# Mixer gate and output projections channel-major, with the gate blocks between the steps of the attention loops and x kept in DRAM meanwhile

## What is computed

```
proj = u @ w_in                      # 1024 -> 256 + 128 + 32 + 2304 + 1024 + 1024
c_q, c_kv, k_rope, qkv, gate_a, gate_b = split(proj)
o_mla = latent attention, 8 heads, all 512 keys per query
o_dil = three groups of windowed attention (dilation 1, 4, 16), 4 heads of 64 each,
        mixed by softmax over the groups' log-sum-exp
merged = sigmoid(gate_a) * (o_mla @ w_o_mla) + sigmoid(gate_b) * (o_dil @ w_o_dil)
y = merged @ w_out
x = x + gate * rms_norm(y, g_post_mix)
```

## Time and profile before

| | |
|---|---|
| median of 3 runs (lowest, highest) | 1302.97 us (1302.61, 1304.91) |
| span of the profiled execution | 1303.2 us |
| PE busy | 1206.4 us, 93% |
| DVE busy | 702.1 us, 54% |
| ACT busy | 508.7 us, 39% |
| mean granted clock of PE | 0.981 |
| chain that ended last, part of PE | 85% |
| mixer, from the last latent turn to the first chunk of w_out | 459.90 to 867.04 us |

### The profile page before, as it was taken

The page is one execution under the profiler, slowest core; times in us unless marked ns, Lnnn a source line. Parts: engine busy times, 40 slices in busy tenths (PEclk is TensorE's granted clock), DMA queues, the critical chain, the costliest instruction groups (busy, mean ns, idle before and its releaser), DMA issues.

```text
span 1303.2 us, 16470 instructions
## 1 busy us (share of the span) xinstructions
PE 1206.4 (93%) x5832; PEld 1013.2 (78%) x5832; DVE 702.1 (54%) x967; ACT 508.7 (39%) x844; POOL 38.7 (3%) x101
## 2 busy tenths in 40 slices
PE   2699999999999879899887799999899999999997
PEld 2688888888888767787777787887788888888885
DVE  6667777334584659923375666247632222226574
ACT  2431222224474547722354732336532222225542
POOL 3000000000010200010000000001100000000000
PEclk9999999999999979999899999999899999999999
DMA  7669999325545100023200213225233333336563
GB/s 310 208 188 280 277 278 282 104 75 183 185 170 186 47 15 25 26 81 98 81 1 1 66 65 116 95 81 177 82 97 97 97 97 97 97 97 193 178 196 111
DMA packets 132765, 167.36 MB, mean 128 GB/s; under 512 B 5735, under 2 KB 100074, under 8 KB 132714
## 3 DMA queue, kind: packets, MB, share of 16 engines
q1 hardware_dynamic: 132714, 166.68, 40.9%
HBM read 164.56 MB, written 2.10 MB: 128 GB/s over the span
## 4 chain that ended last, share of the span: by engine, by line
PE 85%; DVE 8%; ACT 3%; issue 2%; DMA 1%; POOL 0%; SPq 0%; POOLq 0%; ACTq 0%; DVEq 0%
PE ps L1743 27%; PE ps L1744 27%; PE ps L1745 27%; PE ps L1749 3%; DVE mla_pt_lo L1533 1%; DVE stat L1520 1%; DVE mla_p L1527 1%; DVE h_lo L1175 1%; DVE upd L1189 1%; PE ps L2204 1%; DMA x_resid<-in_x 1%; DVE w_lo L1121 1%; ACT h L711 0%; DVE ada_acc L1189 0%; PE ps L1781 0%
## 5 line engine op out<-in xcount | busy, mean ns | idle before, releaser
L1121 DVE TENSOR_TENSOR w_lo<-w_raw,w_hi 128x1024 fp32r<-128x1024 f32 (+2 forms) x240 | 286.2, 1209 | 232.1 <-ACT w_hi L656 228.8
L656 ACT ACTIVATE w_hi<-w_raw 128x1024 fp32r<-128x1024 f32 (+2 forms) x240 | 246.4, 1045 | 243.9 <-PE ps L1745 221.5
L1743 PE MATMUL ps<-h_hi,w_hi 128*128 128x512 f32 (+1 forms) x768 | 289.0, 376 | 10.2 <-DVE h_lo L1175 10.2
L1744 PE MATMUL ps<-h_lo,w_hi 128*128 128x512 f32 (+1 forms) x768 | 287.5, 374 | 0.0
L1745 PE MATMUL ps<-h_hi,w_lo 128*128 128x512 f32 (+1 forms) x768 | 287.5, 374 | 0.0
L1743 PEld LDWEIGHTS ps<-h_hi,w_hi 128*128 128x128 f32 x768 | 147.2, 192 | 36.0 <-DVE h_lo L1175 11.2
L1230 DVE TENSOR_TENSOR a_buf<-silu,ps 128x512 f32 (+1 forms) x44 | 30.3, 688 | 256.3 <-ACT silu L744 256.3
L744 ACT ACTIVATE silu<-ps 128x512 f32<-128x512 f32 x44 | 26.3, 598 | 363.8 <-PE ps L1745 363.8
L1745 PEld LDWEIGHTS ps<-h_hi,w_lo 128*128 128x128 f32 x768 | 147.0, 191 | 25.0
L1744 PEld LDWEIGHTS ps<-h_lo,w_hi 128*128 128x128 f32 x768 | 147.2, 192 | 24.7
L1743 PE MATMUL ps<-w_hi,a_hi 128*128 128x512 f32 x416 | 165.5, 398 | 0.7 <-DVE a_lo L1133 0.7
(11 more groups left out here) (260 smaller groups left out, 1300.3 us busy)
## 6 DMA issues: line engine op xcount, KB each, us to landing
w_raw<-in_w_down SPq DMA_DIRECT2D x88, 512.0 KB, 4.3
ada_raw<-in_w_ada SPq DMA_DIRECT2D x61, 512.0 KB, 5.0
w_raw<-in_w_gate SPq DMA_DIRECT2D x44, 512.0 KB, 3.9
w_raw<-in_w_up SPq DMA_DIRECT2D x44, 512.0 KB, 5.1
w_raw<-in_w_in SPq DMA_DIRECT2D x28, 512.0 KB, 3.6
w_raw<-in_w_out SPq DMA_DIRECT2D x16, 512.0 KB, 3.5
a_buf<-in_w_ada SPq DMA_DIRECT2D x11, 512.0 KB, 10.1
w_raw<-in_w_in SPq DMA_DIRECT2D x8, 384.0 KB, 3.4
```

The source lines that it names most:

```text
L656: act.activation(dst, w_raw[:, slot, 0:width], copy).then_inc(hi_ready, 1)
L1121: dve.tensor_tensor(lo, w_raw[:, slot, 0:width], hi.bitcast(F32), ALU.subtract).then_inc(lo_ready, 1)
L1743: pe.matmul(dst, a_h, b_h, start=start, stop=False, **kw)
L1744: pe.matmul(dst, a_h, b_l, start=False, stop=False, **kw)
```

## The change

The number of products stays the same; where they stand and how they lie changes.

- Gates and both output projections are computed with channels on the partitions: the weights become the stationary operand, a block is 128 channels by 512 tokens, and no transposes of the merged tile remain. Each gate block is 8 products into one PSUM bank, then copied raw to SBUF by ACT; the sigmoids are taken later, in four instructions for each gate.
- Gate a: block 0 stands ahead of the second pair of value tiles, block 1 behind the first key product, blocks 2 to 7 inside the MLA loop, two products per unit in 24 of the units (`GA_FILL`). Key product and query turn of a head now share one bank, one unit apart.
- After the loop: all values of the dilated groups (`N_V`), the o_mla projection with DVE's gating (`N_OM`), group 0 query and key (`N_QK0`), groups 1 and 2 query and key (`N_QK12`).
- Gate b: block 0 ahead of the dilated loop, blocks 1 to 5 inside it (`GB_FILL`), blocks 6 and 7 behind it. The value projection is no longer in this loop. Strided preparations use bank 0 for query and for key in turn.
- Then o_dil by w_o_dil, 16 products; DVE multiplies with sigmoid b and adds gated o_mla block by block.
- `ga` takes the place of x in SBUF. SP stores x to DRAM behind the load of gate block 0, and loads it back in `down(1)` after the first half's weights.
- The SBUF layout is given by hand in one arena.

The core of the diff:

```diff
-        PREP = [("local", 0, 0, 0, 0), ("local", 1, 1, 5, 0), ("strided", 0, 0, 0, 8), ("strided", 1, 0, 3, 16),
-                ("strided", 0, 1, 0, 20), ("strided", 1, 1, 2, 20)]
+        PREP = [("local", 0, 0, (0, 1), 0), ("local", 1, 1, (5, 6), 0), ("strided", 0, 0, (0, 0), 8),
+                ("strided", 1, 0, (0, 0), 16), ("strided", 0, 1, (0, 0), 20), ("strided", 1, 1, (0, 0), 20)]
+        GA_FILL = {u0 + d: 2 for u0 in (0, 6, 12, 18, 24, 31) for d in range(4)}
+        GA_COPY = {3: 2, 9: 3, 15: 4, 21: 5, 27: 6, 34: 7}
+        GA_SPLIT = {2: N_GA + 3, 6: N_GA + 4, 11: N_GA + 5, 16: N_GA + 6, 21: N_GA + 7, 25: N_V, 28: N_V + 1,
+                    31: N_V + 2}
+        GB_FILL = {v0 + d: 2 for v0 in (1, 6, 11) for d in range(4)} | {16: 4, 17: 4, 20: 8}
+        GB_COPY = {4: 1, 9: 2, 14: 3, 17: 4, 20: 5}
+        GB_SPLIT = {2: N_GB + 3, 4: N_GB + 4, 7: N_GB + 5, 12: N_GB + 6, 18: N_GB + 7, 22: N_OD, 24: N_OD + 1}
+        QK12_TILES = (0, 3, 1, 2)
...
+            load_gate(N_GA, OFF_GATE)
+            for t in range(KT):
+                sp.wait_ge(x_new, t + 1)
+                sp.wait_ge(xn_ready, KT + t + 1)
+                sp.wait_ge(x_squared, KT + t + 1)
+                sp.dma_start(x_spill[t * P:(t + 1) * P, :], x[:, t, :]).then_inc(x_spilled, 16)
...
+                    if d == 1 and hf == 0:
+                        sp.wait_ge(m_t_ready, KD)
+                        sp.wait_ge(x_spilled, 16 * KT)
+                        for t in range(KT):
+                            sp.dma_start(x[:, t, :], x_spill[t * P:(t + 1) * P, :]).then_inc(x_back[t], 16)
...
+            def gate_steps(n, bank, ks):
+                for k in ks:
+                    if k == 0:
+                        arrived(n)
+                    i = product(ps[:, bank, :], w(n, k * P, (k + 1) * P), h(k, slice(0, T)), k == 0, k == KD - 1)
+                    if k == KD - 1:
+                        i.then_inc(ga_done if n == N_GA else w_used, 1)
...
+            d_operand(0, 0)
+            d_operand(0, 1)
+            pe.wait_ge(d12_copied_dve, 1)
+            gate_steps(N_GB, 7, range(KD))
...
+                if v in (16, 20):
                     turns_and_values(v)
+                    for i in (3,) if v == 16 else (4, 5):
+                        for m in range(2):
+                            d_operand(i, m)
+                            gate_b_fill(2)
...
+            for j in (6, 7):
+                pe.wait_ge(mix_copied, j - 5)
+                gate_steps(N_GB + j, j - 6, range(KD))
+            pe.wait_ge(od_ready, 1)
+            for j in range(KD):
+                n = N_OD + j // 4
+                if j % 4 == 0:
+                    arrived(n)
+                if j < 4:
+                    pe.wait_ge(gb_copied, KD)
+                    pe.wait_ge(mix_copied, 8)
+                else:
+                    pe.wait_ge(m_t_summed, j - 3)
                 for c in range(2):
+                    i = product(ps[:, j % 4, :], w(n, c * 512 + j % 4 * P, c * 512 + j % 4 * P + P),
+                                (od_hi[:, c, :], od_lo[:, c, :]), c == 0, c == 1)
...
# ACT, behind the dilated loop
+            mix_copies(0)
+            mix_copies(1)
+            for p in range(2):
+                for j in range(2):
+                    act.wait_ge(mix_diff, 2 * p + j + 1)
+                    act.activation(mix[:, p, 2 * j, :], mix[:, p, 2 * j, :], ACT.Exp).then_inc(mix_exp, 1)
+            gate_b_copy(6)
+            split_to(N_OUT)
+            gate_b_copy(7)
+            act.wait_ge(gb_copied, KD)
+            for y in (gb_first[:, :], gb_early[:, :, :], gb_mid[:, :], gb_late[:, :, :]):
+                act.activation(y, y, ACT.Sigmoid).then_inc(sgb_ready, 1)
+            split_to(N_OUT + 1)
+            act.wait_ge(mixed, 2)
+            act.activation(od_hi[:, :, :], u12[:, :, :], copy).then_inc(od_hi_ready, 1)
...
# DVE, behind the dilated loop
+            mix_scales(0)
+            mix_scales(1)
+            mix_outputs(0)
+            mix_outputs(1)
+            dve.wait_ge(od_hi_ready, 1)
+            dve.wait_ge(mixed, 2)
+            dve.tensor_tensor(od_lo[:, :, :], u12[:, :, :], od_hi[:, :, :].bitcast(F32), ALU.subtract)\
+                .then_inc(od_ready, 1)
+            split_to(N_OUT + 1)
+            dve.wait_ge(sgb_ready, 4)
+            for j in range(KD):
...
+                dve.tensor_tensor(gb[j], gb[j], ps[:, j % 4, :], ALU.mult).then_inc(m_t_summed, 1)
+                dve.wait_ge(m_t_summed, j + 1)
+                dve.tensor_tensor(m_t[:, j * T:(j + 1) * T], gb[j], ga[:, j, :], ALU.add).then_inc(m_t_ready, 1)
```

More of the change, by code:

```diff
@@ L295, in encoder_block @@
         m_turned = sem("m_turned")
-        m_qk_hi = sem("m_qk_hi")
-        m_qk_ready = sem("m_qk_ready")
+        m_keyed = sem("m_keyed")
+        m_k_hi = sem("m_k_hi")
+        m_k_ready = sem("m_k_ready")
+        m_q_hi = sem("m_q_hi")
+        m_q_ready = sem("m_q_ready")
+        x_spilled = sem("x_spilled")
+        x_back = [sem(f"x_back{t}") for t in range(KT)]
+        ga_done = sem("ga_done")
+        ga_copied = sem("ga_copied")
+        sga_ready = sem("sga_ready")
+        om_done = sem("om_done")
+        v_done = sem("v_done")
+        qk0_done = sem("qk0_done")
+        qk12_done = sem("qk12_done")
+        gb_copied = sem("gb_copied")
+        sgb_ready = sem("sgb_ready")
+        od_done = sem("od_done")
+        m_t_summed = sem("m_t_summed")
         m_scores = sem("m_scores")
@@ new lines, in _ @@
+            act.activation(om_hi[:, :, :], o_mla[:, :, :], copy).then_inc(om_hi_ready, 1)
+            act.wait_ge(ga_copied, KD)
+            for b in range(4):
+                split_to(N_V + 3 + b)
+                act.activation(ga[:, 2 * b:2 * b + 2, :], ga[:, 2 * b:2 * b + 2, :], ACT.Sigmoid)\
+                    .then_inc(sga_ready, 1)
+            split_to(N_OM + 2)
+            for t in range(KT):
+                if t < KT - 1:
+                    act.wait_ge(v_done, t + 1)
+                else:
+                    act.wait_ge(w_used, N_V + KD)
+                act.activation(v12_hi[:, t, :], ps[:, 2 * t, :], copy).then_inc(v12_hi_ready, 1)
+                act.activation(v0_hi[:, t, :], ps[:, 2 * t + 1, 0:GW], copy).then_inc(v0_hi_ready, 1)
@@ new lines, in _ @@
+            split_to(N_QK12 + 2)
+            for t in range(KT):
+                if t < KT - 1:
+                    act.wait_ge(qk0_done, t + 1)
+                else:
+                    act.wait_ge(w_used, N_QK0 + KD)
+                act.activation(qk0[:, t, :], ps[:, 2 + t, :], copy).then_inc(d0_copied, 1)
+            split_to(N_GB + 2)
+            for t in (0, 1):
+                act.wait_ge(qk12_done, QK12_TILES.index(t) + 1)
+                act.activation(qk12[:, t, :, :], ps[:, 2 * t:2 * t + 2, :], copy).then_inc(d12_copied_act, 1)
@@ L973, in d_operands, with gate_b_copy @@
+            def gate_b_copy(j):
+                act.wait_ge(w_used, N_GB + j + 1)
+                if 1 <= j < 5:
+                    act.wait_ge(d_turned, 4)
+                if j == 5:
+                    act.wait_ge(d12_rotated, KT)
+                if j >= 6:
+                    act.wait_ge(d_scores, len(D_UNITS))
+                bank = 7 if j == 0 else 1 if j < 6 else j - 6
+                act.activation(gb[j], ps[:, bank, :], copy).then_inc(gb_copied, 1)
             def d_operands(i):
-                kind, g, _, bank, before = PREP[i]
@@ L980, in d_operands @@
                     act.wait_ge(kz_clear, 4)
[L981 to L983 removed]
+                parts = [(dq_hi[:, g, :], ps[:, banks[0], :], DIL_SCALE)]
+                parts += [(kz_hi[a * E:a * E + E, g, a, :], ps[a * E:a * E + E, banks[1], :], 1.0) for a in range(2)]
+                for m, (dst, src, scale) in enumerate(parts):
+                    if m == 1:
+                        act.wait_ge(d_turned, 2 * i + 2)
                     if kind == "strided":
@@ L2076, in _ @@
                     if k == 0:
-                        pe.wait_ge(d0_copied, t + 1)
-                        pe.wait_ge(v0_ready, t + 1)
+                        pe.wait_ge(v12_ready, 2 + t // 2)
+                        pe.wait_ge(v0_ready, 2 + t // 2)
+                    i = product(ps[:, 2 + t, :], h(k, slice(t * P, (t + 1) * P)), w(n, 0, 2 * GW), k == 0, k == KD - 1)
+                    if k == KD - 1 and t < KT - 1:
+                        i.then_inc(qk0_done, 1)
+                i.then_inc(w_used, 1)
+            for k in range(KD):
+                n = N_QK12 + k
+                arrived(n)
+                for t in QK12_TILES:
+                    if k == 0:
+                        pe.wait_ge(*((om_gated, KD), (d0_copied, 2), (d0_copied, 4), (v0_ready, KT))[t])
                     for b in range(2):
```

670 lines of the change are left out of this document (308 added, 362 removed).

## The result

The changed kernel is slower: 1306.61 us (median of 12 runs, 1304.90 to 1307.46) against 1302.66 (12 runs, 1298.06 to 1304.91). The ratio is 1.0036, with a 95% interval of 1.0023 to 1.0048. The profiled execution has a span of 1304.7 us beside 1303.2 before. Forecast: 1280.

What follows compares the result with a forecast made beforehand. Taken as the bound: PE, busy 93% of the span, where its queue stands still or its clock is low. Terms summed to 22.8 us off 1303.2, giving 1280.4; forecast 1271 to 1290 (chance 0.64), wider range 1265 to 1297.

Steps and rivals of the forecast that it cites:

- Item 5: Dilated loop: 99.1 us plus 5.5 becomes 91, with PE's own work 77.5 and the rest waits; gain 13.6 us.
- Item 2: MLA loop: takes in 48 products (33.1 us) and grows from 82.1 to 109.9 us, PE covering DVE's added splits.
- The bound of 104.6: Dilated loop: upper bound on its time in us within Item 5, if today's waits all stay.
- Rival (b): Both loops: fills are not absorbed, each loop grows by its fill in full (115.2 and 104.6); 1299 us, chance 0.11.
- (c): MLA loop: beyond Rival (b), 0.90 us hand-off bubbles on all 24 filled units, 16.2 us more; 1315 us, chance 0.07.
- Item 3: Dense stretch between the loops: 176 products, 121.7 us, plus 0.5 of waits, 122.2 in all; gain 0.9 us.
- Items 1, 4 and 6: Ahead of MLA loop 19.4 us, ahead of dilated loop 6.5, behind it 37.2 (loss 13.0, PE idle 12.1).
- Item 7: Mixer's down projection: gain 2.4 us from dropped turns and a wait, 0.5 taken for reloading x; net 1.9.
- The table load: Dilated loop, within Item 5: a Sigmoid adds two reloads, 1.28 us each; the second costs nothing, or 1.3 if uncovered.

Runs made afterwards that it cites:

- e1: Changed kernel with the seven weight splits taken out of the dilated loop and run behind it, its 40 products kept; loop 97.9 us against 115.7.
- e5: Changed kernel with DVE taking the low half of each dilated-loop split one unit later than ACT the high half; loop 108.1 us against 115.7.
- e10: e7 with the eight weight splits of the MLA loop moved behind it, its 48 products kept; MLA loop 104.8 us against 109.0.
- e8: e3 with the value projection of groups 1 and 2 loading 128 neighbouring tokens instead of strided ones; that stage 33.7 us (changed kernel 37.4).
- e3: Changed kernel with two gate-b blocks in the dilated loop, five behind it, four splits at the loop's end; 1290.56 us, ratio 0.9905 to the kernel before.
- e12: e9 with three gate-b blocks in the dilated loop instead of two and one split early, at unit 5; 1285.64 us, ratio 0.9877, loop 97.4.
- e6: e3 with its four dilated-loop splits at units 2, 5, 7 and 12 instead of 23, 25, 26 and 27; loop 104.4 us against 94.9.
- e7: e3 with strided preparations over two banks, DVE splitting each key half at once, one key turn a unit earlier; 1279.68 us, ratio 0.9829.
- e9: e7 with DVE taking the low half of every in-loop weight split one unit later, in both loops; 1278.46 us, ratio 0.9826.

## Why the prediction was wrong

**Item 5, the step that failed.** The sum there was PE's own work at nearly full clock, 77.5, plus 13.5 of waits. Measured: 86.4 busy and 29.6 waiting. Of the 25 us, 16.1 are waits and 8.9 is PE's own time at a clock of 0.90. e1 ran the same products in 78.7 at 0.98, so the 77.5 was right, and the fills do bring the clock up, but only where the waits are short. The sum of the waits failed. By PE's rows:

| PE's waits, us | forecast | changed kernel | e1, no splits |
|---|---|---|---|
| copies of values, in the drain above all | 7.1 | 10.8 | 8.3 |
| low parts of queries and keys | 6 | 8.0 | 6.2 |
| probabilities and the rest | 0.4 | 6.4 | 1.3 |
| copies of gate blocks | 0 | 4.1 | 3.3 |

- The term put at nothing without a reason is the splits of gate and projection weights. Item 2 names its eight and lets PE cover them; item 5 doesn't mention its seven. With them out of the loop 17.8 of the 25 us are gone: 10.4 of waits, through hand-offs of every kind, and 7.4 of PE's time (e1). Of the waits, 4.1 are DVE standing for ACT's half (e5).
- The second such term is the copies of gate blocks as a condition for PE's next block: 4.1 us, 3.3 without splits. The prediction counted the copies in the MLA loop as work of ACT and put no wait for them here.
- The preparations through one bank were priced at 6 us and were nearly right: 8.0, and 6.2 without the splits.

Five splits stood in this loop before as well, and DVE waited 4.4 us for them. So the 17.8 is the price of all seven, and no run shows what the two more cost by themselves, or the five among fills. The bound of 104.6, "today's waits stay", was no bound: waits of 19.1 us became 29.6 though fills stood in them. That is the sign the prediction named for being wrong, that the waits the fills replace come back beside them. Rival (b) rested on the same mistake, and (c) put its bubbles in the MLA loop, where they didn't come. No rival held a term for work added on ACT and DVE inside the dilated loop, so the range ended at 1297.

**Item 2** was right to 1 us, and in the main for its reason: e10 gives the eight splits 4.2 us, 0.8 of them waits. (Its 31 units add up to 73.0 us in the rows, 550.51 less 477.47, and not to 72.7; this moves 0.1 us.)

**Item 3** missed by 3.0: the strided weight loads (3.7, e8), taken there at the price of plain ones. A row of the kernel before would have told it; these are its loads for the same strided products, then still in the dilated loop:

```profile
L1744 PEld LDWEIGHTS ps<-w_lo,h_hi 128*128 128x128 f32 x33 | 10.5, 317 | 0.3
```

**Items 1, 4 and 6** came out to 0.2 us, the last with the gap as forecast (12.1):

```profile
857.81 0.79 PE L1798 MATMUL ps<-od_hi,w_hi 128*128 128x512 f32 x1 [12.24 <-DVE od_lo L1769]
```

Behind the gap the granted clock was 0.56 for 5.8 us, which is some 2.5 us of loss where 3 had been added. (Not every such gap is followed by it: PE's idle time of 9.55 us up to 37.0 in the kernel before has a clock of 1.00 ahead of it and behind it.) e3 shows that this gap was not the price of the change, only of where the blocks stood: five blocks behind the loop cover it for 1.5 us more of that stretch.

**Item 7** gained 3.1 instead of 1.9, or 2.7 when both kernels are cut at the first matmul of w_out (867.24 and 871.42). The reload takes 7.5 us from issue to landing, the half microsecond for it was not needed:

```profile
x_resid<-x_spill SPq DMA_DIRECT2D x4, 512.0 KB, 7.5
```

**The table load.** ACT's rows behind the loop's start, the exponential directly at the end of the load, and DVE's row of the maximum that this exponential needs:

```profile
719.22 1.28 ACT L1072 ACT_TABLE_LOAD   x1
720.52 0.51 ACT L1072 ACTIVATE dil_p<-dil_p,dil_nm 128x256 f32<-128x256 f32 x1
```

```profile
719.43 0.42 DVE L1673 TENSOR_REDUCE dil_nm<-dil_p 128x1 f32<-128x256 f32 x1
```

The drain of 1.38 us that the Trainium skill ("ScalarE: Activation LUTs", "What ACT_TABLE_LOAD costs") adds to each switch is not seen between the load and the activation here. The load did stand ahead of the first exponential, whose maximum was there at 719.85, and held it for 0.7 us. Whether the loop became longer by that no run tried.

**Open.** What the 7.4 us of busy time in the 17.8 are owed to. They are clock: cut into windows of 1 us, the changed loop shows five stretches at the lower level (granted 0.50), each of which begins within or just behind one of PE's waits of 3.05, 2.91, 3.61, 2.18 and 4.09 us. The first of these rows and the last:

```profile
734.68 0.80 PE L1798 MATMUL ps<-h_hi,w_hi 128*128 128x512 f32 x1 [3.05 <-ACT gb_early L1046]
...
817.52 0.55 PE L1798 MATMUL ps<-dpt_hi,v_hi 128*128 128x256 f32 x1 [4.09 <-ACT u L1101]
```

By these windows they cost PE 9.6 us; e1 has one such stretch, 1.6 us. So the low clock goes with the waits that the splits bring, but e3 and e8 differ in it by 4.0 us with the same waits, and no run held it fixed.

## What to carry to other kernels

When work is moved into a loop of hand-offs between engines, price all of it on the queue of every engine it touches: here 40 matmul products more or 35 fewer moved the loop by 10.4 and 3.4 us, while the seven weight splits, of which five had stood there before, cost 17.8 us, where the whole change was to gain 22.8. A product is cheap only where PE has gaps: in the fullest part of the loop it is paid in full (e12). A step of two engines, each with its queue in a fixed order, costs the second engine the wait as well: issue its half a unit later (4.1 us of waits less in e5), and put such steps where the loop drains (3.8 less in e3 than in e6). Then look at what the moved work takes away, a PSUM bank as well as time. With blocks, splits and banks placed so, the same change is 1.7% faster than the kernel before (e7, e9), not 0.4% slower.
